# Splits moved from GpSimd to VectorE, memory rows asked for earlier, and a new timetable for cached values, in a decoder step

## The chip, the cores and the metric

One core of one Trainium2 chip. The metric is the device time of one execution, in microseconds (us). Five engines matter: TensorE (PE, matrix products; PEld is its weight loads), VectorE (DVE), ScalarE (ACT), GpSimd (POOL), and the sync engine (SP), which only issues transfers. ACT and POOL issue transfers too. Each engine works through its own list in order; semaphores tie the lists together.

## The reference, cut to what matters

The reference is one inference step of a one-layer hybrid decoder, for a prompt of 1,024 positions and for eight sample sequences of one new position each, with shared weights. Model width is 1,024, and there are four head groups of 256 columns.

```python
z = rmsnorm(x, g) @ w_in            # columns split among the groups below
outs = (fox(q, k, v, logf),         # A: causal, 4 heads of 64, decay bias
        sgu(u, v),                  # B: gated position mixing in chunks of 128
        dilated(q, k, v, rel_bias), # C: 3 dilated windows, 4 heads
        mem_attend(q, mk, mv))      # M: 4 heads into 256 memory tokens
x = x + merge_groups(outs) @ w_out
x = x + conv_ffn(rmsnorm(x, g))     # w_up, causal conv of width 3, silu gate, w_down
```

The memory keys and values are `rmsnorm(mem) @ w_mem_kv`. For each sample sequence, group A also reads 4,096 cached keys and values, 32 pages of 128 rows that a page table names; C reads 320 cached rows per sequence, and M 256. All data are float32.

## The kernel before, in words

**Products in three parts.** A float32 product is made of three products of "hi" and "lo" parts: `whi*hhi + wlo*hhi + whi*hlo` (lines 856 to 858, and 1035 to 1037 in the feed-forward part). ACT writes the hi part (a copy that rounds), another engine the lo part (value minus hi part).

**Stage 1, projection (0 to about 362 us).** Six column blocks of weights, 0 to 4 of `w_in` and 5 of `w_mem_kv`, each of eight chunks of 128 rows. PE works through units `(b, tt)`: block b with `tt` = "S" (the samples) or 0 to 7 (128 prompt positions), and (5, 0) and (5, 1) for the memory rows. Chunk q = 8b + kc is loaded by SP (`w_load`, line 454, which waits until chunk q - 4 is split, since there are four staging buffers), its hi part is made by ACT (`split_hi`, 1136) and its lo part, for q of 8 and more, by POOL (`split_lo`, 2162). `chunk_turns` (323) puts chunks 0 to 3 of block b at units (b-1, 0) to (b-1, 3) and chunks 4 to 7 all at (b-1, 7), where the units of that block free their slots. Beside this DVE normalises the q and k heads (`reduce_sq`, `finish_norm`, 1561, which waits for an inverse root from POOL), gates group B (`gate`, 1597), and multiplies cached keys by the sample queries (`k_dot`, lines 1546 and 1549, one "granule" of four pages at a time). A ring of four slots holds the granules of keys; SP and ACT load two pages each in this stage (`load_pages`, 353; lines 356 and 357 are the reading of a page number and the transfer). The memory rows (`memT`) are loaded in pairs at units (4, 2) to (4, 5) by `x_load` (462), which waits for the pair before to be split; ACT makes their hi part (1156), DVE their lo part (1520).

**Stage 2, attention (about 362 to 735 us).** 96 steps g, eight to a head: 0 to 31 causal heads, 32 to 63 memory heads, 64 to 95 dilated heads. A step is one block of 128 queries: PE makes the logits (931, 932), DVE adds a bias and takes the maximum (1795), ACT the exponential (`ex`, 1277), PE transposes (941, 946), ACT and DVE copy to SBUF (1289, 1811), PE multiplies with the values (957), and DVE divides (1820). In steps 0 to 15 DVE also has the last 16 key granules, whose four pages SP loads alone.

The cached values are summed by PE in between. `v_sum(k)` (961, matmuls at line 976) takes granule k of 74: 64 of four pages for A, and ten for C and M, loaded with one transfer each. They pass through a ring of four slots, so that granule k can be loaded once `v_sum(k - 4)` is done. `v_step` (414) is the timetable: which step has which granule. POOL's list is one loop over k (`v_load`, 2191): all four pages for k under V0, else two, and the other two come from SP at the step of `v_sum(k - 4)` (`V_PAIR`, 437; 617).

```python
V0, V1, V2 = 8, 28, 44      # granules 0-7: steps 4-15; 8-27: 16-31; 28-43: 32-63; 44-73: 64-86
```

POOL's loop also has four maxima over partitions (`max_all`, 2148) at fixed k and, at k = 66, an inverse root that waits for the squares of step 79 (`rs_o`). DVE waits for the second maximum in `subtract_a(1)` at step 19 (1643); its own part of that maximum is written in step 16.

**Stage 3 (735 us to the end).** Output projection and feed-forward part, with PE busy throughout; the change touches nothing in it.

Of the kernel before, what the change touches and what calls it, by code (L numbers as in the profile page):

```python
# [97 lines left out]
def build(nc, t):  # L98
# [5 lines left out]
    with ctx:  # L104
# [308 lines left out]
        V0, V1, V2 = 8, 28, 44  # L413
        v_step = [4 + k * 12 // V0 for k in range(V0)] + [16 + (k - V0) * 16 // (V1 - V0) for k in range(V0, V1)] + \
# [14 lines left out]
        def v_total(k):  # L429
            return sum(64 if n < V0 else 32 if n < NVA else 16 for n in range(k % 4, k + 1, 4))  # L430

        def v_total_sp(k):
            return sum(32 for n in range(k % 4, min(k + 1, NVA), 4) if n >= V0)
# [4 lines left out]
        for k_ in range(V0, NVA):  # L438
            V_PAIR.setdefault(v_step[k_ - 4], []).append(k_)
# [11 lines left out]
        def _(sp):  # L451
# [63 lines left out]
            for u, k in enumerate(units):  # L515
                b, tt = k
                for q in CT_load[u]:
                    w_load(q)
# [16 lines left out]
                if b == 4 and tt != "S" and tt >= 2 and tt < 6:  # L535
                    for i in (2 * (tt - 2), 2 * (tt - 2) + 1):
                        x_load(16 + i)
# [74 lines left out]
            for g in range(STEPS):  # L612
# [4 lines left out]
                for k in V_PAIR.get(g, ()):  # L617
                    sp.wait_ge(S("v_used"), k - 3)
                    load_pages(sp, vpool, k // 8, k % 8, k % 4, (2, 3), vring, "vs_ld")
# [515 lines left out]
        def _(act):  # L1135
# [187 lines left out]
            for g in range(STEPS + 4):  # L1323
# [8 lines left out]
                if g < STEPS:  # L1332
                    ex(g)
                if g == 2:
                    samp_exp(0)
# [137 lines left out]
        def _(dve):  # L1473
# [214 lines left out]
            for u, k in enumerate(units):  # L1688
                b, tt = k
                if b == 4 and tt != "S" and tt >= 2 and tt < 6:  # L1690
# [14 lines left out]
                if pending:  # L1705
                    finish_norm(pending)
                    pending = None
                for n in grans:
# [419 lines left out]
        def _(pool):  # L2128
# [33 lines left out]
            def split_lo(q):  # L2162

                pool.wait_ge(S("w_hi"), q + 1)
                pool.tensor_tensor(wlo[:, q % NW, 0:WID[q // KC]], wst[:, q % 4, 0:WID[q // KC]],  # L2165
                                   whi[:, q % NW, 0:WID[q // KC]].bitcast(f32), ALU.subtract).then_inc(S("w_split"), 1)
# [6 lines left out]
            for u, k in enumerate(units):  # L2173
                for bb, kc in CT[u]:
                    split_lo(bb * KC + kc)
# [15 lines left out]
            def v_load(k):  # L2191
                if k >= 4:
                    pool.wait_ge(S("v_used"), k - 3)
                if k < NVA:
                    load_pages(pool, vpool, k // 8, k % 8, k % 4, range(4) if k < V0 else (0, 1), vring, "vr_ld")
# [6 lines left out]
            for k in range(NV):  # L2202
                if k == 17:
                    max_all(2, 0, 16, 32)
                if k == 38:
                    max_all(3, 1, 0, 32)
                if k == 43:
# [72 lines left out]
```

## Time and profile before

| | |
|---|---|
| time before, three runs | 1625.07 us median (1620.05 to 1626.87) |
| the profiled execution's own time | 1638.29 us |
| its span, first to last instruction | 1635.5 us |
| granted TensorE clock, mean | 0.912 of full speed |
| busy: PE, PEld, DVE, ACT, POOL | 89%, 81%, 59%, 28%, 15% |
| moved by DMA | 172.90 MB, mean 106 GB/s |

The profiled execution took 13.2 us more than the median of the unprofiled ones. Times in the trace are counted from the first instruction. In a timeline row stand start, duration, engine, source line, operation, written and read tiles; in brackets how long the engine stood idle before it, and what ended that. `PE L856` is TensorE at line 856. PEclk is the granted clock of TensorE as a share of 2.4 GHz.

### The profile page before, as it was taken

The page shows a single profiled execution, that of the slowest core. Times are in us where ns is not written, and L with a number is a line of the kernel's source. Part 1 is how long each engine was busy: PE and PEld are TensorE (multiplying, and loading weights), DVE is VectorE, ACT ScalarE, POOL GpSimd, SP SyncE. Part 2 cuts the span into 40 slices and gives each one's busy share as a digit, 9 for nine tenths or more (in the row PEclk, how much of TensorE's full clock was granted, in tenths as well). Part 3 has the DMA queues.
Part 4 walks back from the last instruction along what each step waited for, and adds up shares of the span by engine and source line. Part 5 has one row for each costly group of instructions (what it writes and reads, how often), then busy time and mean ns, then how long its engine had stood idle before and what let it go on. Part 6 is the DMA issues. An engine that isn't in the chain of part 4 may idle for free.

```text
span 1635.5 us, 25981 instructions
## 1 busy us (share of the span) xinstructions
PE 1463.0 (89%) x8745; PEld 1320.4 (81%) x8745; DVE 959.1 (59%) x1490; ACT 461.9 (28%) x720; POOL 238.2 (15%) x293
## 2 busy tenths in 40 slices
PE   6985989746889798787989999999999999999997
PEld 4774777635666566577989999999999999999997
DVE  6566568646855856383456664555645556454653
ACT  5213112223334444452232321222212222221210
POOL 5533146142123213300000000000000000000000
PEclk8998989866678758898999999999999999999999
DMA  6277546437566846521300211202111020120202
GB/s 207 94 244 220 164 127 194 142 111 217 166 201 190 273 116 202 178 74 45 131 26 1 78 39 39 66 14 78 34 46 65 14 79 16 63 66 14 78 1 114
DMA packets 124745, 172.90 MB, mean 106 GB/s; under 512 B 22869, under 2 KB 97646, under 8 KB 124194
## 3 DMA queue, kind: packets, MB, share of 16 engines
q1 hardware_dynamic: 102864, 134.49, 26.2%
q0 software_dynamic: 8384, 24.13, 5.0%
q10 hardware_dynamic: 13354, 12.47, 2.5%
q8 instruction: 78, 1.28, 0.3%
q14 instruction: 65, 0.53, 0.1%
HBM read 157.09 MB, written 16.91 MB: 106 GB/s over the span
## 4 chain that ended last, share of the span: by engine, by line
PE 65%; DVE 7%; issue 6%; SPq 4%; DMA 3%; POOL 2%; ACT 2%; POOLq 0%; ACTq 0%; DVEq 0%; PEldq 0%
PE ps L1035 16%; PE ps L1036 16%; PE ps L1037 16%; PE ps L957 4%; SPq L356 2%; PE ps L856 2%; PE ps L858 2%; PE ps L857 2%; PE ps L976 2%; SPq L357 1%; DMA vring<-in_cache_a_v 1%; PE ps L941 1%; PE ps L908 1%; PE ps L932 1%; DVE ring L1546 1%
## 5 line engine op out<-in xcount | busy, mean ns | idle before, releaser
L1035 PE MATMUL ps<-hhi,uhi 128*128 128x344 f32 x1056 | 339.5, 322 | 12.4 <-DVE ulo L1996 5.0
L1036 PE MATMUL ps<-hlo,uhi 128*128 128x344 f32 x1056 | 338.7, 321 | 2.7 <-issue 2.7
L1037 PE MATMUL ps<-hhi,ulo 128*128 128x344 f32 x1056 | 338.1, 320 | 0.0
L1035 PEld LDWEIGHTS ps<-hhi,uhi 128*128 128x128 f32 x1056 | 199.7, 189 | 14.3 <-issue 11.2
L1036 PEld LDWEIGHTS ps<-hlo,uhi 128*128 128x128 f32 x1056 | 199.7, 189 | 3.9 <-issue 3.9
L1037 PEld LDWEIGHTS ps<-hhi,ulo 128*128 128x128 f32 x1056 | 199.7, 189 | 0.0
L856 PE MATMUL ps<-whi,hhi 128*128 128x512 f32 (+1 forms) x376 | 152.8, 406 | 44.7 <-POOL wlo L2165 31.0
L1035 PE MATMUL ps<-ahi,dhi 128*128 128x344 f32 x528 | 170.4, 323 | 3.6 <-DVE dlo L2121 3.6
L1036 PE MATMUL ps<-alo,dhi 128*128 128x344 f32 x528 | 170.5, 323 | 0.0
L1037 PE MATMUL ps<-ahi,dlo 128*128 128x344 f32 x528 | 169.7, 321 | 0.0
L2050 DVE TENSOR_TENSOR uu<-ps,rstd_bc 128x1032 f32<-128x1032 f32 x44 | 54.3, 1233 | 183.8 <-PE ps L1037 183.7
L957 PEld LDWEIGHTS ps<-vst,pts 128*128 128x128 f32 x704 | 107.8, 232 | 62.8 <-issue 33.8
L857 PE MATMUL ps<-wlo,hhi 128*128 128x512 f32 (+1 forms) x376 | 148.2, 394 | 0.0
L858 PE MATMUL ps<-whi,hlo 128*128 128x512 f32 (+1 forms) x376 | 148.0, 394 | 0.0
L957 PE MATMUL ps<-vst,pts 128*128 128x65 f32 x704 | 121.1, 323 | 20.4 <-DVE oN L1820 20.2
L856 PEld LDWEIGHTS ps<-whi,hhi 128*128 128x128 f32 x376 | 76.7, 204 | 65.4 <-POOL wlo L2165 34.9
L2083 DVE TENSOR_TENSOR x<-ps,x 128x1032 f32<-128x1032 f32 x80 | 98.3, 1229 | 13.0 <-PE ps L1037 10.7
L1546 DVE TENSOR_TENSOR ring<-ring,qb 128x1024 f32<-128x1024 f32 x64 | 83.0, 1297 | 38.4 <-DMA ring<-in_cache_a_k 38.4
L357 POOL DMA_DIRECT2D vring<-in_cache_a_v x144 | 77.9, 541 | 185.9 <-issue 163.2
L1035 PEld LDWEIGHTS ps<-ahi,dhi 128*128 128x128 f32 x528 | 100.2, 190 | 5.5 <-DVE dlo L2121 3.9
L1037 PEld LDWEIGHTS ps<-ahi,dlo 128*128 128x128 f32 x528 | 100.2, 190 | 0.0
L1036 PEld LDWEIGHTS ps<-alo,dhi 128*128 128x128 f32 x528 | 100.2, 190 | 0.0
(243 smaller groups left out, 2361.2 us busy)
## 6 DMA issues: line engine op xcount, KB each, us to landing
fst<-in_w_upL SPq DMA_DIRECT2D x44, 512.0 KB, 3.7
ring<-in_cache_a_k SPq DMA_DIRECT2D x168, 128.0 KB, 2.4
vring<-in_cache_a_v POOLq DMA_DIRECT2D x144, 128.0 KB, 3.0
vring<-in_cache_a_v SPq DMA_DIRECT2D x112, 128.0 KB, 2.7
ring<-in_cache_a_k ACTq DMA_DIRECT2D x88, 128.0 KB, 2.7
fst<-in_w_down SPq DMA_DIRECT2D x22, 512.0 KB, 3.6
wst<-in_w_in SPq DMA_DIRECT2D x32, 256.0 KB, 4.3
x<-in_xT SPq DMA_DIRECT2D x16, 258.0 KB, 4.9
```

Source lines behind the costliest of these rows:

```text
L356: page = sp.value_load(ptab[0:1, bass.ds(seq * PAGES + (group * 4 + j), 1)], min_val=0, max_val=NPOOL - 1)
L357: sp.dma_start(dst[:, slot, j, :], pool[bass.ds(page, 1)].rearrange("o p c -> p (o c)"))\
L856: pe.matmul(out, lh, whi[:, sl, 0:w], start=(kc == 0), stop=False)
L857: pe.matmul(out, lh, wlo[:, sl, 0:w], start=False, stop=False)
L858: i = pe.matmul(out, ll, whi[:, sl, 0:w], start=False, stop=(kc == KC - 1))
L957: i = pe.matmul(ps[:, 6, 0:HD + 1], pts[:, g % 2, j, :], vst[:, hp % 2, j, H % 2, :], start=(j == 0), stop=(j == nb - 1))
L1035: pe.matmul(out, lhs_hi(kc), rhs_hi(kc)[:, cs], start=(n == 0), stop=False)
L1036: pe.matmul(out, lhs_hi(kc), rhs_lo(kc)[:, cs], start=False, stop=False)
L1037: i = pe.matmul(out, lhs_lo(kc), rhs_hi(kc)[:, cs], start=False, stop=(n == nk - 1))
L1546: dve.tensor_tensor(kv, kv, q.broadcast_to([P, 4, WG]), ALU.mult).then_inc(S("k_mul"), 1)
L2050: dve.tensor_tensor(c3(uu[:, :]), U3(k % 2), c3(rstd_bc[:, :]), ALU.mult).then_inc(S("f_free"), 1)
L2083: dve.tensor_tensor(c3(x2[:, d, :]), U3(d % 2), c3(x2[:, d, :]), ALU.add).then_inc(S("f_free"), 1)
```

## The change

Three things. The lo parts of weight chunks 8 to 47 are made by VectorE, at the start of the unit, and in a block's last unit behind `finish_norm`. SP asks for the memory rows at the head of units (4, 2) to (4, 5), ahead of the weights. The timetable of cached values becomes: granules 0 to 11 in steps 4 to 15, 12 to 25 in steps 16 to 31, 26 to 33 in steps 32 to 63, 34 to 73 in steps 64 to 86; for granules 0 to 11 POOL loads two pages and ACT the other two, those of granules 0 to 3 in step 0. POOL's third and fourth maximum come at k = 33 and 36.

```diff
-        V0, V1, V2 = 8, 28, 44
-        v_step = [4 + k * 12 // V0 for k in range(V0)] + [16 + (k - V0) * 16 // (V1 - V0) for k in range(V0, V1)] + \
+        V0, V1, V2 = 12, 26, 34
+        v_step = [4 + k for k in range(V0)] + [16 + (k - V0) * 16 // (V1 - V0) for k in range(V0, V1)] + \
...
-        for k_ in range(V0, NVA):
-            V_PAIR.setdefault(v_step[k_ - 4], []).append(k_)
+        for k_ in range(NVA):
+            V_PAIR.setdefault(max(v_step[k_ - 4], 3) if k_ >= 4 else 0, []).append(k_)
... sync engine, projection
             for u, k in enumerate(units):
                 b, tt = k
+                if b == 4 and tt != "S" and tt >= 2 and tt < 6:
+                    for i in (2 * (tt - 2), 2 * (tt - 2) + 1):
+                        x_load(16 + i)
                 for q in CT_load[u]:
                     w_load(q)
...
-                if b == 4 and tt != "S" and tt >= 2 and tt < 6:
-                    for i in (2 * (tt - 2), 2 * (tt - 2) + 1):
-                        x_load(16 + i)
... sync engine, attention
                 for k in V_PAIR.get(g, ()):
-                    sp.wait_ge(S("v_used"), k - 3)
-                    load_pages(sp, vpool, k // 8, k % 8, k % 4, (2, 3), vring, "vs_ld")
+                    if k >= V0:
+                        sp.wait_ge(S("v_used"), k - 3)
+                        load_pages(sp, vpool, k // 8, k % 8, k % 4, (2, 3), vring, "vs_ld")
... scalar engine, attention
                 if g < STEPS:
                     ex(g)
+                for n in V_PAIR.get(g, ()):
+                    if n < V0:
+                        if n >= 4:
+                            T_.wait("v_used", n - 3)
+                        load_pages(act, vpool, n // 8, n % 8, n % 4, (2, 3), vring, "vs_ld")
... vector engine, projection
                 b, tt = k
+                if tt != NT - 1:
+                    for bb, kc in CT[u]:
+                        split_lo(bb * KC + kc)
...
                 if pending:
                     finish_norm(pending)
                     pending = None
+                if tt == NT - 1:
+                    for bb, kc in CT[u]:
+                        split_lo(bb * KC + kc)
                 for n in grans:
                     granule(n)
... gpsimd
             for u, k in enumerate(units):
-                for bb, kc in CT[u]:
-                    split_lo(bb * KC + kc)
...
-                    load_pages(pool, vpool, k // 8, k % 8, k % 4, range(4) if k < V0 else (0, 1), vring, "vr_ld")
+                    load_pages(pool, vpool, k // 8, k % 8, k % 4, (0, 1), vring, "vr_ld")
...
-                if k == 38:
+                if k == 33:
                     max_all(3, 1, 0, 32)
-                if k == 43:
+                if k == 36:
                     max_all(4, 2, 0, 32)
```

## Rows read from the trace of the kernel before

**Rows 1.** Busy time by stretch: from:to, length, busy (count) by engine, PEclk, DMA share, GB/s

```profile
50.00:362.00 312.00, 254.94 (x1142) 206.55 (x1141) 194.42 (x273) 64.65 (x129) 118.33 (x106) 0.89 0.54 165
395.00:453.00 58.00, 47.57 (x290) 36.99 (x291) 50.06 (x99) 22.10 (x39) 11.37 (x22) 0.71 0.58 172
453.00:476.00 23.00, 18.11 (x120) 13.57 (x119) 10.46 (x34) 6.76 (x10) 6.88 (x14) 0.77 0.81 231
476.00:520.00 44.00, 42.15 (x315) 31.48 (x315) 22.15 (x74) 20.66 (x37) 13.96 (x26) 0.81 0.55 172
520.00:609.00 89.00, 76.28 (x427) 53.38 (x423) 61.53 (x145) 42.96 (x122) 18.67 (x35) 0.70 0.67 202
609.00:671.00 62.00, 55.54 (x473) 40.53 (x473) 36.12 (x105) 32.82 (x67) 19.27 (x36) 0.91 0.65 194
880.00:1635.00 755.00, 738.75 (x4664) 734.40 (x4663) 423.58 (x503) 165.11 (x151) 0.00 (x0) 1.00 0.15 49
640.00:660.00 20.00, 17.40 (x156) 12.64 (x156) 12.21 (x36) 12.01 (x27) 8.85 (x16) 1.00 0.89 277
```

**Rows 2.** Waits of PE, 50 to 362 us: total, times, longest

```profile
PE ps L856 <- POOL wlo L2165: 31.0, 6, 14.3
PE ps L856 <- DVE zn L1570: 8.4, 2, 4.6
```

**Rows 3.** Splits by source line: DVE's eight of block 0, and POOL's 40 (min/median/max ns)

```profile
L1511 DVE TENSOR_TENSOR wlo<-wst,whi x8: 677/684/1777, 8.3 to 28.2; 128x512 fp32r<-128x512 f32 x8
L2165 POOL TENSOR_TENSOR wlo<-wst,whi x40: 725/1287/2275, 53.0 to 345.6; 128x512 fp32r<-128x512 f32 x32, 128x260 fp32r<-128x260 f32 x8
```

**Rows 4.** Timelines of DVE, POOL, ACT and PE around the ends of blocks

```profile
130.50 6.60 POOL L2165 TENSOR_TENSOR wlo<-wst,whi 128x512 fp32r<-128x512 f32 x4 [17.41 <-ACT whi L1145]
196.97 0.85 DVE L1605 SCALAR_TENSOR_TENSOR ob<-ps,prm_b,zo 128x64 f32<-128x64 f32 x4
339.45 0.19 POOL L2144 TENSOR_SCALAR rsn<-ssn 128x4 f32<-128x4 f32 x1 [7.62 <-issue]
340.83 0.48 DVE L1570 SCALAR_TENSOR_TENSOR zn<-ps,rsx,rsn 128x256 f32<-128x256 f32 x1 [5.67 <-POOL rsn L2147]
342.10 0.80 PE L856 MATMUL ps<-whi,hhi 128*128 128x512 f32 x1 [14.31 <-POOL wlo L2165]
```

**Rows 5.** SP's timeline at unit (4, 3)

```profile
289.37 0.42 SPq L501 DMA_DIRECT2D scr_q<-zo  x1
296.81 0.91 SPq L472 DMA_DIRECT2D xst<-in_memT  x2
```

**Rows 6.** Issues of pages by queue (min/median/max ns), and ScalarE's pair

```profile
L357 POOL DMA_DIRECT2D vring<-in_cache_a_v x144: 538/538/740, 360.5 to 657.0; - x144
144.45 1.44 ACTq L357 DMA_DIRECT2D ring<-in_cache_a_k  x2
493.50 0.54 POOL L357 DMA_DIRECT2D vring<-in_cache_a_v  x1 [0.62 <-issue]
```

**Rows 7.** DVE's timeline, steps 3 and 15

```profile
392.34 1.23 DVE L1546 TENSOR_TENSOR ring<-ring,qb 128x1024 f32<-128x1024 f32 x1 [10.89 <-DMA ring<-in_cache_a_k]
450.23 1.23 DVE L1546 TENSOR_TENSOR ring<-ring,qb 128x1024 f32<-128x1024 f32 x1 [2.38 <-DMA ring<-in_cache_a_k]
```

**Rows 8.** DVE and POOL around step 19

```profile
456.17 0.16 DVE L1640 TENSOR_TENSOR small<-small 8x16 f32<-8x16 f32 x1
473.88 0.39 POOL L2150 PARTITION_ALL_REDUCE small<-small  x1 [7.37 <-issue]
474.31 0.90 DVE L1648 TENSOR_TENSOR sA<-sA,small 128x128 f32<-128x128 f32 x4 [6.58 <-POOL small L2150]
```

**Rows 9.** PE's value sums: two that waited, and one at full clock

```profile
622.29 1.03 PE L976 MATMUL ps<-vring,sA 128*4 128x256 f32 x8 [3.18 <-DMA vring<-in_cache_a_v]
643.48 0.61 PE L976 MATMUL ps<-vring,sA 128*4 128x256 f32 x8
679.15 1.04 PE L976 MATMUL ps<-vring,sC 96*4 96x256 f32 x8 [7.77 <-DMA vring<-in_cache_c_v]
```

More of the change, by code:

```diff
@@ L429, in v_total @@
         def v_total(k):
-            return sum(64 if n < V0 else 32 if n < NVA else 16 for n in range(k % 4, k + 1, 4))
+            return sum(32 if n < NVA else 16 for n in range(k % 4, k + 1, 4))
         def v_total_sp(k):
-            return sum(32 for n in range(k % 4, min(k + 1, NVA), 4) if n >= V0)
+            return sum(32 for n in range(k % 4, min(k + 1, NVA), 4))
         def k_total(n):
@@ L2160, in x_add @@
                 pool.tensor_tensor(sacx[:, c], sacx[:, c], (sqt0 if i % 2 else sqt1)[:, :], ALU.add).then_inc(S("x_acc"), 1)
[L2162 to L2166, printed above, removed]
             for i in range(8):
```

## The prediction

> **What bounds the kernel now.** I read the table by stretches first. After 880 us TensorE is busy 738.75 of 755 us at full clock [rows 1]; the change touches nothing there, so what happens before has to be worth the difference. From 50 to 362 us (projection) TensorE is busy 254.9 of 312 us, and the list of its waits gives 31.0 us to the lo parts that GpSimd makes and 8.4 us to VectorE's normalising [rows 2]. In attention the bound changes by stretch [rows 1]: steps 4 to 15 (395 to 453 us) belong to VectorE, busy 50.1 of 58; steps 20 to 31 (476 to 520) and 64 to 79 (609 to 671) belong to TensorE, 42.2 of 44 and 55.5 of 62; the memory steps (520 to 609) to TensorE and VectorE in turn, 76.3 and 61.5 of 89, at a mean clock of 0.70, between its levels of 1.2 and 2.4 GHz. Three single waits stand out in the timelines: VectorE 10.89 us at step 3 for key pages [rows 7], VectorE 6.58 us at step 19 for a maximum from GpSimd [rows 8], TensorE 7.77 us at step 80 for a value granule [rows 9].
>
> **Projection: the splits.** The change moves 40 splits: 32 of 512 columns at 0.684 us on VectorE instead of 1.287 on GpSimd [rows 3], and 8 of 260 columns, which no VectorE row shows; I take half, 0.35. That is 32 x 0.684 + 8 x 0.35 = 24.7 us more for VectorE, busy 194.4 of 312 us [rows 1]. The splits for kc 0 to 3 fall in units where it has slack; I cost them at nothing. If the cover were gone, 16 x 0.684 + 4 x 0.35 = 12.3 us would show.
>
> The four chunks at a block's end do show. GpSimd needed 6.60 us for four [rows 4], VectorE needs 2.7; but in blocks 0, 3 and 4 they now stand behind `finish_norm`, some 2 us of VectorE work that itself waits for GpSimd's inverse root. So the first chunk comes later and the last one earlier. For the memory block: GpSimd is held by the first maximum over partitions until 339.45 (7.62 us of idle "issue" before its next row), VectorE gets its root and starts at 340.83, and the first split ends at 340.83 + 0.5 + 0.9 + 0.7 = 342.9; TensorE resumed at 342.10 [rows 4]. **Nearly all of the 14.3 us wait, the largest of the 31.0, therefore stays**, with another name on it. Its last chunk comes at 345 instead of 346.9: -1. Block 0 +1, block 3 0, block 1 (no `finish_norm`, first chunk as late as now, last 2 earlier) -2. In block 2 the four splits enter ahead of a gate that TensorE stands waiting for (VectorE row at 196.97 [rows 4]): +2.7. Ends of blocks: about +1.
>
> **Projection: the memory rows.** SP had nothing to do after 289.8 and asked for the second pair at 296.81 [rows 5], because the weight ahead of it waited for a split. Without that it goes out as soon as the first pair is split: up to 7 us earlier, of which VectorE's own added splits (four of block 3's end and two more) take some 3. I take -4, out of 0 to -7, and it comes off the 8.4 us wait and what follows it. Projection: **-3**.
>
> **Steps 0 to 15.** ScalarE gets 24 page issues. A pair takes 1.44 us from first to last [rows 6], so a page costs 1.44 - 0.35 = 1.1. Eight in step 0: 8.8 us, which delay the second exponential and with it the third bias row, but behind these VectorE waits 10.89 us for keys anyway [rows 7]: nothing. Queued behind the other 16 (2.2 us in each of steps 4 to 11) are ScalarE's copies and exponentials; it is busy 22.1 of 58 us, 39.7 with them, and VectorE stays the longer [rows 1]: +1. Four more sums on TensorE (4 x 0.97, below) fit beside VectorE: nothing. On SP the value pairs of steps 10 and 11, which stood ahead of the last key loads, go to steps 12 and later: the 2.38 us key wait of step 15 goes [rows 7]. Together **-1**.
>
> **Steps 16 to 31.** GpSimd reaches the second maximum after loading granule 16, for which it needs `v_sum(12)`: at step 19 now, at step 16 with the new timetable. VectorE's part was written at 456.17; the maximum came at 473.88, after 7.37 us of "issue" that start only when GpSimd gets there; VectorE waited until 474.31 [rows 8]. New: 456.3 + 7.4 + 0.4 = 464.1, and VectorE reaches its wait at about 462.7: 1.5 us are left of 6.6, so -5. Six sums fewer (20 to 14). One takes 0.61 us at full clock (0.55 until the next instruction) and 1.03 at half (0.97) [rows 9]; TensorE is the bound at a clock of 0.81: 6 x 0.75 = -4.5. Without the stop, less of the stretch runs at 1.2 GHz: -1.5. Together **-11**.
>
> **Memory steps.** Eight sums fewer. About three fall where VectorE's products of cached rows set the pace, and count nothing; five count 0.97: **-5**.
>
> **Dilated steps.** Granules 34 to 63 are due in steps 64 to 80, where 44 to 65 were. Four lie ready; 26 must come. GpSimd issues a page every 0.54 + 0.62 = 1.16 us [rows 6], two per granule: 26 x 2.32 = 60.3, plus about 4.6 until the last one lands and 3 for unevenness: 68 us against 62. TensorE by itself: 55.5 + 9 x 0.55 = 60.5 [rows 1, 9], so the loads are the bound and the sums hide behind them: +6. Now the stop at step 80: granule 66 waits behind an inverse root that needs step 79. Its sum moves from step 80 to 82; that gives two steps of about 3.2 us: of 7.77 us [rows 9] 1.5 stay, -6. Dilated: **0**.
>
> The page "DMA: Bandwidth & Descriptors" of the Trainium skill says under "Issuing engines are not separate DMA queues" that all queues run on the same 16 DMA engines, so that one more issuing engine saves only sequencer time. By this rule ScalarE's 24 issues bring no value earlier; I credited them with nothing, so the sum is the same, but the rule makes a rival, below.
>
> **Sum.** -3 - 1 - 11 - 5 + 0 = -20. The profiled execution took 1638.3 us, 13.2 over the median of 1625.1: 1618 of 1638, and taken off the median **1605 us**.
>
> **Rivals.**
>
> *A. The maximum stays late* (chance 0.14). The step -5 - 1.5 fails if GpSimd's 7.4 us land behind more loads, or if the granules it then loads late stop TensorE in steps 21 to 23. For it: from 464.1 each of three granules takes 2.3 us and is due within 3 us. Against: four slots are filled before. 1605 + 6.5 = 1612.
>
> *B. ScalarE's issues are exposed* (0.13). They sit between exponentials on a chain from VectorE to TensorE and back. If nothing hid them, 24 x 1.1 = 26 us; half of that gives 1617, all of it 1630. For it: in steps 4 to 7 ScalarE would be busy some 4.7 us of a step of 4.5. Against: VectorE's 50.1 of 58.
>
> *C. Dilated heads bound by transfers* (0.12), the case on the slower side. Thirty granules of 524 KB are 15.7 MB, plus some 2.5 MB for the next heads. In 68 us that is 268 GB/s; the trace shows 277 in one stretch of 20 us, 194 over the whole of steps 64 to 79 [rows 1]. If a granule took 3.3 us, as over steps 16 to 31 (67 us for 20), these steps would last 30 x 3.3 = 99 us: +37 instead of +6, thus 1605 + 31 = 1636. It decides from (62 + 26 + 8) / 30 = 3.2 us a granule, 26 being what the rest gains. For it: waits of 3.18 us already stand there [rows 9]. Against: GpSimd held 2.3 us a granule for eight granules at 277 GB/s. The rule cited above is what this rival rests on beside the rows: three queues, but one set of engines.
>
> *D. More clock* (0.06). The memory steps have a clock of 0.70 and the projection 0.89; if the stops vanish and 2.4 GHz holds, another 15 us go: 1590.
>
> **Chances and range.** Forecast 0.55 (its own range 1596 to 1612). What a measurement of this kernel can tell from no change is about 0.5%, 8.1 us: faster is under 1617, slower over 1633. Forecast and D are faster; of A 0.11 faster, 0.03 the same; of B 0.01, 0.09 and 0.03 slower; of C 0.03 the same and 0.09 slower. Faster 0.73, same 0.15, slower 0.12. Range: downwards the unknown costs (memory rows -3 more, step 19 -2, memory steps -3, part of D) reach 1592; upwards A and most of B are to be held (hidden splits +12, issues +13): 1627.
>
> **What would show it.** No PE wait on GpSimd's splits; a wait of some 14 us at the memory block under VectorE's name; the second `xst` issue within 3 us of the first pair's split; the second maximum some 8 us after step 16's row and VectorE's wait at step 19 under 3 us; steps 16 to 31 in about 56 us instead of 67; the memory steps in 84 instead of 89; steps 64 to 79 in about 68 with GpSimd issuing without a gap; the wait at `vring<-in_cache_c_v` under 2 us. Wrong if VectorE waits for ScalarE in steps 4 to 11 by more than 5 us in sum, or if steps 64 to 79 take over 75 us.

## The result, and the profile after

The changed kernel takes **1635.1 us** (median of 12 runs, 1631.5 to 1644.5) beside 1627.5 us of the kernel before on the same chip (12 runs, 1620.1 to 1631.0): ratio **1.0055, interval 1.0034 to 1.0076**. It is slower, by about 9 us; 1605 was forecast. The profiled execution has a span of 1642.9 us (before 1635.5) and a mean clock of 0.907 (before 0.912).

The table by stretches, cut at the starts of steps 4, 16, 32, 64, 74, 80 and 87 (a step starts with VectorE's first instruction on its logits); columns as in [rows 1]:

```profile
50.00:362.00 312.00, 251.09 (x1145) 204.98 (x1143) 207.02 (x315) 67.59 (x133) 66.78 (x68) 0.90 0.55 167
390.59:444.78 54.19, 43.68 (x302) 31.79 (x306) 49.70 (x98) 22.31 (x39) 12.02 (x22) 0.79 0.73 217
444.78:494.52 49.74, 48.86 (x404) 37.71 (x400) 32.85 (x106) 27.07 (x47) 15.49 (x29) 0.92 0.72 219
494.52:587.51 92.99, 85.42 (x371) 63.61 (x368) 62.11 (x146) 43.06 (x121) 9.49 (x18) 0.53 0.48 144
587.51:627.44 39.93, 34.59 (x320) 23.20 (x313) 24.93 (x68) 19.15 (x34) 17.70 (x33) 0.97 0.76 220
627.44:661.48 34.04, 28.04 (x205) 21.25 (x209) 11.34 (x37) 14.04 (x33) 11.67 (x21) 0.75 0.71 209
661.48:712.05 50.57, 36.04 (x235) 25.80 (x229) 16.53 (x48) 15.12 (x26) 10.41 (x10) 0.66 0.38 105
```

TensorE's waits, 50 to 362 us, against [rows 2]: the low parts still hold it, now under VectorE's name; the positional gate (`ob`) and the forget row (`crow`) hold it longer than before (6.2 and 5.5 us).

```profile
PE ps L857 <- DVE wlo L1517: 30.2, 3, 15.5
PE ps L832 <- DVE ob L1611: 9.2, 3, 4.4
PE ps L832 <- DVE crow L1750: 9.0, 1, 9.0
```

The timelines that answer to [rows 4] (memory block), [rows 8] (steps 16 to 19) and [rows 9] (here step 82); `osqj` is ScalarE's square of step 79, which the inverse root waits for:

```profile
338.69 0.19 POOL L2156 TENSOR_SCALAR rsn<-ssn 128x4 f32<-128x4 f32 x1 [7.41 <-issue]
340.99 2.49 DVE L1517 TENSOR_TENSOR wlo<-wst,whi 128x512 fp32r<-128x512 f32 x4
341.73 0.79 PE L857 MATMUL ps<-whi,hhi 128*128 128x512 f32 x1 [15.55 <-DVE wlo L1517]
...
455.56 0.39 POOL L2162 PARTITION_ALL_REDUCE small<-small  x1 [7.18 <-issue]
458.68 0.89 DVE L1654 TENSOR_TENSOR sA<-sA,small 128x128 f32<-128x128 f32 x4
...
659.65 0.40 ACT L1319 ACTIVATE osqj<-oN 128x256 f32<-128x256 f32 x1
659.64 1.49 POOL L383 DMA_DIRECT2D vring<-in_cache_c_v  x2
670.31 0.20 POOL L2156 TENSOR_SCALAR rso<-sso 128x24 f32<-128x24 f32 x1 [9.19 <-issue]
679.07 1.04 PE L977 MATMUL ps<-vring,sC 96*4 96x256 f32 x8 [5.67 <-DMA vring<-in_cache_c_v]
```

Where the time went, by the starts of steps in the two traces: step 0 starts 2.6 us earlier than before, step 16 7.8, step 32 25.0 and step 74 still 22.8 us earlier. Then it is lost: step 80 is 9.4 us earlier, step 87 is 4.8 us later, and the last instruction 7.4. **Steps 64 to 86 take 124.5 us, before 97.9.**

That 97.9 is itself high. The profiled execution before was 13 us over its median and has in step 67 a stop that is longer than in any other trace (11.57 us for the step; 8.02 and 6.62 in e3 and e4, about 4 to 5 in the rest). The two versions below with the old timetable take 92.9 and 92.7 us for steps 64 to 86. So the dilated heads lost about 32 us, where I had forecast none.

### The profile page after: what moved, and what is told of

The parts are those of the page before. It is cut to its first block, busy times and chain, and to the rows that moved or that the text cites. A ratio compares the mean times of both kernels' runs of the same rounds, so it can differ in the third digit from the quotient of the medians.

```text
span 1642.9 us, 25988 instructions
## 1 busy us (share of the span) xinstructions
PE 1465.6 (89%) x8745; PEld 1325.1 (81%) x8745; DVE 970.6 (59%) x1530; ACT 462.9 (28%) x720; POOL 177.7 (11%) x237
## 3 DMA queue, kind: packets, MB, share of 16 engines
q1 hardware_dynamic: 101712, 133.44, 25.9%
## 4 chain that ended last, share of the span: by engine, by line
PE 65%; DVE 8%; issue 6%; SPq 5%; DMA 3%; POOL 2%; ACT 1%; POOLq 0%; ACTq 0%; DVEq 0%; PEldq 0%
PE ps L1036 17%; PE ps L1037 16%; PE ps L1038 16%; PE ps L958 4%; SPq L356 2%; SPq L357 2%; PE ps L977 1%; PE ps L857 1%; PE ps L858 1%; PE ps L859 1%; PE ps L942 1%; PE ps L933 1%; DVE ring L1552 1%; DMA vring<-in_cache_a_v 1%; PE ps L909 1%
## 5 line engine op out<-in xcount | busy, mean ns | idle before, releaser
L2062 DVE TENSOR_TENSOR uu<-ps,rstd_bc 128x1032 f32<-128x1032 f32 x44 | 54.2, 1233 | 188.2 <-PE ps L1038 188.2
L958 PEld LDWEIGHTS ps<-vst,pts 128*128 128x128 f32 x704 | 108.5, 233 | 52.8 <-issue 34.7
L857 PEld LDWEIGHTS ps<-whi,hhi 128*128 128x128 f32 x376 | 75.7, 201 | 57.1 <-DVE wlo L1517 38.2
L2095 DVE TENSOR_TENSOR x<-ps,x 128x1032 f32<-128x1032 f32 x80 | 98.3, 1229 | 14.3 <-PE ps L1038 11.9
L357 POOL DMA_DIRECT2D vring<-in_cache_a_v x128 | 69.4, 542 | 198.3 <-issue 177.4
L1552 DVE TENSOR_TENSOR ring<-ring,qb 128x1024 f32<-128x1024 f32 x64 | 78.0, 1219 | 17.0 <-DMA ring<-in_cache_a_k 16.9
```

The lines of the kernel that those rows point to most:

```text
L357: sp.dma_start(dst[:, slot, j, :], pool[bass.ds(page, 1)].rearrange("o p c -> p (o c)"))\
L857: pe.matmul(out, lh, whi[:, sl, 0:w], start=(kc == 0), stop=False)
L958: i = pe.matmul(ps[:, 6, 0:HD + 1], pts[:, g % 2, j, :], vst[:, hp % 2, j, H % 2, :], start=(j == 0), stop=(j == nb - 1))
L1552: dve.tensor_tensor(kv, kv, q.broadcast_to([P, 4, WG]), ALU.mult).then_inc(S("k_mul"), 1)
L2062: dve.tensor_tensor(c3(uu[:, :]), U3(k % 2), c3(rstd_bc[:, :]), ALU.mult).then_inc(S("f_free"), 1)
L2095: dve.tensor_tensor(c3(x2[:, d, :]), U3(d % 2), c3(x2[:, d, :]), ALU.add).then_inc(S("f_free"), 1)
```

## The experiments

Lengths in us of groups of steps in each run's trace, with the granules of values in the dilated heads, and the time as a ratio to the kernel before, timed beside it on the same chip (95% interval in brackets; e1 to e4, e5 to e8, e9 to e12, e13 to e16 and e17 to e18 share a chip each):

| version | granules | 4-15 | 16-31 | 32-63 | 64-73 | 74-79 | 80-86 | ratio |
|---|---|---|---|---|---|---|---|---|
| before | 20 | 57.6 | 66.9 | 89.8 | 40.9 | 20.6 | 36.4 | 1 |
| after | 30 | 54.2 | 49.7 | 93.0 | 39.9 | 34.0 | 50.6 | 1.0055 |
| e1 | 20 | 56.2 | 49.6 | 84.5 | 34.5 | 23.3 | 37.6 | 0.9892 (0.9843-0.9940) |
| e2 | 30 | 57.1 | 49.2 | 89.6 | 39.6 | 34.6 | 46.8 | 1.0077 (1.0046-1.0107) |
| e3 | 20 | 58.0 | 68.9 | 84.2 | 36.6 | 20.1 | 36.2 | 1.0039 (1.0005-1.0072) |
| e4 | 20 | 57.5 | 68.5 | 87.1 | 35.0 | 19.9 | 37.8 | 0.9955 (0.9929-0.9981) |
| e5 | 20 | 56.1 | 50.7 | 86.8 | 35.4 | 21.7 | 38.9 | 0.9844 (0.9795-0.9893) |
| e6 | 30 | 60.0 | 49.3 | 88.8 | 42.0 | 32.8 | 40.1 | 1.0007 (0.9984-1.0030) |
| e7 | 30, half the bytes | 56.5 | 49.3 | 88.5 | 45.2 | 23.7 | 47.4 | 0.9972 (0.9946-0.9998) |
| e8 | 30 | 56.5 | 49.6 | 90.0 | 55.4 | 34.7 | 48.0 | 1.0144 (1.0106-1.0182) |
| e9 | 30, no pages | 56.0 | 49.4 | 91.6 | 34.3 | 25.9 | 44.7 | 0.9895 (0.9852-0.9938) |
| e10 | 30, a quarter of the sums of 24 of them | 55.1 | 50.5 | 89.3 | 40.0 | 34.6 | 47.8 | 1.0016 (0.9990-1.0041) |
| e11 | 20 | 56.8 | 49.6 | 86.7 | 33.6 | 21.7 | 37.7 | 0.9813 (0.9768-0.9858) |
| e12 | 30 | 55.7 | 49.3 | 89.3 | 42.2 | 35.4 | 47.2 | 1.0017 (0.9992-1.0042) |
| e13 | 30, half the requests | 55.2 | 50.1 | 88.4 | 34.1 | 34.3 | 43.9 | 0.9995 (0.9966-1.0024) |
| e14 | 20 | 55.6 | 49.4 | 88.6 | 35.9 | 26.5 | 27.7 | 0.9718 (0.9677-0.9760) |
| e15 | 16 | 56.0 | 50.5 | 88.0 | 30.5 | 20.1 | 21.9 | **0.9675** (0.9637-0.9714) |
| e16 | 30 | 54.1 | 48.9 | 90.5 | 42.5 | 32.3 | 47.6 | 1.0018 (0.9997-1.0039) |
| e17 | 12 | 54.7 | 49.9 | 95.4 | 30.3 | 19.0 | 25.5 | 0.9741 (0.9697-0.9784) |
| e18 | 16 | 56.1 | 49.9 | 83.7 | 30.5 | 20.4 | 21.7 | 0.9718 (0.9684-0.9752) |

How far one trace can be trusted can be read there too: nine executions with the same projection start step 0 between 358.1 and 364.7 us. A difference of three microseconds in a single trace says nothing. The changed kernel's own trace is the latest of the nine; their mean is 361.8, and 367.4 in the kernel before.

**1. Which part of the change costs.** The changed kernel with the dilated heads' share of before (e1), and each of the three parts alone on the kernel before (e2, e3, e4; their diffs are parts of the change's own).

```diff
 e1, on the changed kernel
-        V0, V1, V2 = 12, 26, 34
+        V0, V1, V2 = 12, 28, 44
-                if k == 33:        # third maximum
+                if k == 38:
-                if k == 36:        # fourth maximum
+                if k == 43:
```

> The changed kernel with V0, V1, V2 = 12, 28, 44 and the last two maxima back ahead of granules 38 and 43: the dilated heads get 20 granules and the memory heads 16, as before the change; all else of the change stays. Theory 1 (the dilated heads are overloaded: 30 granules where 20 were): step 64 starts 20 to 22 us earlier than before the change, steps 64 to 86 take the 97.9 us of before instead of 124.5, and the time is 18 to 22 us under the kernel before (ratio 0.987 to 0.989). Theory 2 (TensorE's granted clock takes back later whatever the early steps gain): steps 64 to 86 still take 115 us or more, and the time is within 6 us of the kernel before (ratio 0.996 to 1.004).

> The kernel before with the new timetable alone (12, 26, 34, ScalarE's page issues, the maxima ahead of granules 33 and 36); splits stay on GpSimd and memory rows behind the weights. Theory 1 (the timetable alone makes the loss): step 4 starts within 1 us of the kernel before (395.1), steps 4 to 31 gain about 20, steps 64 to 86 lose about 26, and the time is 10 to 14 us over the kernel before (ratio 1.006 to 1.009). Theory 3 (the splits on VectorE or the earlier memory rows cost what the timetable gains): the time is under the kernel before.

> The kernel before with only the 40 splits moved to VectorE. By the prediction's terms: ends of blocks +1, the wait of 14.3 us at the memory block stays under VectorE's name; time within 3 us of the kernel before (ratio 0.998 to 1.002). If VectorE's 24.7 us more are not hidden: 12 us over it (ratio 1.007).

> The kernel before with only the memory rows asked for ahead of the weights. By the prediction's term: step 0 starts 4 us earlier (0 to 7), time 1 to 5 us under the kernel before (ratio 0.997 to 0.999), since the attention behind it can take some back. Rival: nothing, because the weight that is now asked for behind the rows comes late in their place.

e1 takes 1605.6 us, by the ratio 18 less than the kernel before, and steps 64 to 86 take 95.4 us. The mean clock is the highest of these four (0.927): the clock takes back nothing that was gained early, and theory 2 is out. e2 has the whole loss, 1.0077. By ratios of 1626 us the parts alone are +12.5 (timetable), +6.3 (splits) and -7.3 (rows), in sum +11.5 beside the +9 of the change.

Both projection terms were off. In e4 SP asks for the second pair of memory rows at 285.46 instead of 296.81 [rows 5], and step 0 starts 10.6 us earlier. In e3 the price was not the amount of VectorE's work (it is busy 203 of the 306 us from 50 to 356), but its **order**: a split stands at the head of a unit and waits for ScalarE's high part, and what TensorE needs waits behind it. VectorE's timeline around the forget row, first e3, then e4:

```profile
159.97 0.69 DVE L1511 TENSOR_TENSOR wlo<-wst,whi 128x512 fp32r<-128x512 f32 x1 [3.60 <-ACT whi L1145]
...
162.96 0.27 DVE L1744 TENSOR_TENSOR crow<-ps,crow 32x128 fp32r<-32x128 f32 x1
```

```profile
159.65 0.28 DVE L1738 TENSOR_TENSOR crow<-ps,crow 32x128 fp32r<-32x128 f32 x1 [2.48 <-ACT crow L1256]
```

In e4 the split is in GpSimd's list, and VectorE waits for nothing but the row's own input. From before to e3 TensorE's waits grow by 3.5 us for the row, 3.0 for the gates, 1.8 for the bias (0.8 to 2.6) and 0.7 for the low parts, and shrink by 2.5 for the normalised rows and 0.4 for the queries: 6.1 in all, against 6.3 by the ratio. But the traces do not show that this reaches the end of the stage: SP asks for the first pair of memory rows at 290.10 in e3 and 285.74 before, 4.4 us late, and step 0 starts only 0.2 us late. So the rows show what waits, the ratio what it costs, and the way from one to the other stays open.

**2. Whether the gains add up, and what stops TensorE at steps 80 to 86.** The splits go back and e1's timetable stays (e5); and, on the changed kernel, one tiny instruction makes GpSimd change its program early (e6).

```diff
 e6
                 if k == 36:
                     max_all(4, 2, 0, 32)
+                    pool.wait_ge(S("gmax"), 4)
+                    pool.tensor_scalar(rso[32:64, 35:36], nhalf[32:64, 0:1], 1.0, 0.0, ALU.mult, ALU.add).then_inc(S("pool_chain"), 1)
+                    chain[0] += 1
                 if k == 66:
+                    pool.wait_ge(S("pool_chain"), chain[0])
```

> Memory rows ahead of the weights and the timetable with V0, V1, V2 = 12, 28, 44 (20 granules in the dilated heads), splits back on GpSimd: what the first four runs say is good, and nothing else. If the gains add up (step 0 10 us earlier as in the run with the rows alone, and from there the 27 us of the run with more in the memory heads): step 0 at 357, step 87 at 667 to 672, time 23 to 28 us under the kernel before (ratio 0.983 to 0.986). Rival: the splits on VectorE were part of that gain, then no better than the 0.989 of that run.

> The changed kernel with one tiny TENSOR_SCALAR on GpSimd right behind its last maximum over partitions, 100 us before the inverse root of the outputs. Theory 4 (the 9.19 us of idle issue ahead of the inverse root at 670.31 are GpSimd's change from one kind of program to the other, which starts only when it gets there, since ScalarE's square was done at 660.2): the root starts within 1 us of the last load ahead of it (661), the next cached rows are asked for at 666 instead of 675, the wait of 5.67 us at step 82 goes, steps 81 to 86 take some 10 us less than 43, time 7 to 12 us under the changed kernel (ratio to before 0.998 to 1.001). Rival (the idle time is the queue or the transfers): it stays over 7 us.

e5: 1604.2 us, ratio 0.9844, within what was expected if the gains add up (step 87 at 675.6 is 4 us later than expected). e6's mechanism was right as well: the 9.19 us of idle ahead of the inverse root are gone, they stand (7.13) in front of the tiny instruction, where nobody waits, and the cached rows go out in time. GpSimd in e6:

```profile
572.00 0.18 POOL L2215 TENSOR_SCALAR rso<-nhalf 32x1 f32<-32x1 f32 x1 [7.13 <-issue]
...
662.22 1.49 POOL L383 DMA_DIRECT2D vring<-in_cache_c_v  x2
663.78 0.20 POOL L2156 TENSOR_SCALAR rso<-sso 128x24 f32<-128x24 f32 x1
...
668.25 1.52 POOL L383 DMA_DIRECT2D vring<-in_cache_c_v  x2
```

Steps 80 to 86 fall from 50.6 to 40.1 us (other versions with 30 granules and their value pages: 46.8 to 48.0, and 43.9 in e13), the time from 1.0055 to 1.0007. So GpSimd idles when it goes from a maximum over partitions to arithmetic or back, with page requests in between or not: 7.62 and 7.37 us in [rows 4, 8], 5.6 to 10.2 in the runs. Where the program is already there, the second maximum starts 1.12 to 1.15 us after VectorE's release (six versions below).

The Trainium skill's page "GPSIMD Engine Reference", section "2.1 Instruction dispatch", has a load of code of about 6 us at the first call of a freshly loaded kernel, with no instruction to be seen in the profile. The trace agrees in that no instruction shows, and the size here is 5.6 to 10.2 us; that the idle time is such a load no run shows.

How exposed this is depends on when GpSimd gets there. In the kernel before it had made its last request by 662.99 and then waited for step 79 as well:

```profile
669.36 0.19 ACT L1318 ACTIVATION_READ_ACCUMULATOR osqj<-oN 128x1 f32 x1
670.37 0.20 POOL L2144 TENSOR_SCALAR rso<-sso 128x24 f32<-128x24 f32 x1 [7.38 <-ACT osqj L1318]
```

The square is done at 669.55 and the root starts 0.82 us later: change of program and wait lie side by side. In the changed kernel the square is done at 660.15, GpSimd gets there at 661.13, and the 9.19 us stand alone.

**3. What is late in steps 64 to 79: the sums, the bytes or the requests.** Five versions of the changed kernel (the semaphore totals that go with each edit are not shown).

```diff
 e7: SP's two pages of granules 34 to 63 left out
-                    if k >= V0:
+                    if V0 <= k < V2:
 e8: GpSimd one page, SP three
+  (2, 3) if k < V2 else (1, 2, 3)          # SP
+  (0, 1) if k < V2 else (0,)               # GpSimd
 e9: no pages for granules 34 to 63, on both queues
+                if V2 <= k < NVA:
+                    pass
 e10: one matmul of four for granules 40 to 63
+                    if q == 3 or not 40 <= k < NVA:
 e13: one request for two neighbouring pages, from each queue
+            page = (4 * k + j) % (NPOOL - 2)
+            eng.dma_start(vring[:, k % 4, j:j + 2, :], vpool[page:page + 2].rearrange("o p c -> p o c"))
```

> The changed kernel without SP's two pages of each granule in the dilated heads (30 granules, 60 pages, 7.9 MB); TensorE sums what lies in the slots. Left out: half of the cached values of granules 34 to 63, so that the rows of the samples are not the reference's. Theory 5 (transfers bind: 216 GB/s and half as much again in peaks): steps 64 to 86 fall from 124.5 to under 108 us. Theory 6 (GpSimd's own issues bind, 1.155 us a page and two pages a granule): GpSimd asks as often as ever, steps 64 to 86 stay within 5 us of 124.5.

> The changed kernel, but in the dilated heads GpSimd asks for one page of each granule and SP for three; the bytes stay. Theory 6 (GpSimd's issues bind): steps 64 to 86 fall under 112 us. Theory 5 (transfers bind): they stay over 119 us. If neither is the bound but the ring of four slots, each to be summed before it is asked for again, both runs give about half of the gain.

> The changed kernel without the pages of granules 34 to 63 on both queues (120 pages, 15.7 MB); TensorE sums old values in the slots, and all waits but those for these pages stay. Left out: the cached values of the dilated heads' 30 granules, so the rows of the samples are not the reference's. If late pages cause the loss (issue, transfer or ring, whichever): steps 64 to 79 take 56 to 60 us instead of 74, with TensorE's clock near 1.0, and steps 64 to 86 take 95 to 105 us instead of 124.5. If the 10 more sums themselves cause it: steps 64 to 86 stay over 115 us.

> The changed kernel with one of the four matmuls of each value sum for granules 40 to 63 (steps 67 to 80); all pages are loaded and waited for. Left out: three quarters of these sums, so the rows of the samples are not the reference's. 24 granules of 0.41 to 0.73 us less is 10 to 17 us less work for TensorE. If late pages set the pace: steps 64 to 86 fall by less than 5 us from 124.5. If TensorE's own work does: by 10 us or more.

> The changed kernel, but for granules 34 to 63 each queue asks once for two neighbouring pages (at fixed places of the cache) instead of twice for one: the same 15.7 MB, 60 requests instead of 120. The rows of the samples are not the reference's, since other pages are summed. Theory 6 (the requests set the pace): steps 64 to 79 take 58 to 64 us instead of 74, near the 60.2 of the run without loads, and the time falls by 10 us or more (ratio to before 0.999 or less). Theory 5 (the transfers do): steps 64 to 79 stay over 70 us.

Late pages are the cause: without them (e9) steps 64 to 86 take 104.9 us, and the time is 26 us under the changed kernel's. With a quarter of the sums of granules 40 to 63 (e10) they take 122.4: the sums do hide, as forecast.

e7 (116.2 us for steps 64 to 86) decided for neither theory, e8 (138.1) met the words of "transfers bind" with the bytes unchanged, and e13 (68.4 for steps 64 to 79) fell between its two cases, since I had asked of the whole stretch. Split at step 74 the runs agree. The rows of steps 64 to 73 and 74 to 79, in e7:

```profile
584.09:629.27 45.18, 37.93 (x324) 26.46 (x321) 24.97 (x67) 19.26 (x34) 18.62 (x35) 0.85 0.50 145
629.27:652.98 23.71, 20.95 (x205) 15.26 (x202) 11.34 (x37) 13.87 (x33) 10.11 (x20) 1.00 0.37 108
```

in e9:

```profile
584.94:619.20 34.26, 33.97 (x324) 24.30 (x321) 24.92 (x68) 18.84 (x34) 0.00 (x0) 0.95 0.24 62
619.20:645.15 25.95, 24.00 (x205) 17.82 (x201) 11.23 (x37) 14.07 (x34) 1.51 (x2) 0.87 0.10 28
```

and in e13, with four microseconds of the second stretch:

```profile
581.52:615.65 34.13, 33.05 (x324) 23.50 (x321) 24.93 (x68) 18.84 (x34) 12.97 (x18) 0.99 0.84 265
615.65:649.94 34.29, 27.20 (x205) 20.34 (x201) 11.25 (x38) 14.20 (x34) 7.26 (x10) 0.80 0.70 223
...
620.00:624.00 4.00, 0.40 (x7) 0.14 (x8) 0.84 (x3) 1.23 (x3) 0.00 (x0) 0.89 1.06 363
```

**Steps 64 to 73 are held by the requests.** Half of them bring the stretch from 39.9 to 34.1 us, as fast as no pages at all (34.3), and move 265 GB/s instead of 220; half the bytes bring nothing (45.2). In the changed kernel GpSimd asks from 589.7 to 632 us every 1.16 us, never idle for more than 0.9. SP, too, needs 17.52 us for 16 pages, 1.10 each:

```profile
606.90 17.52 SPq L357 DMA_DIRECT2D vring<-in_cache_a_v  x16
```

In e8 SP has three pages of each granule, 3.3 us, and the stretch takes 55.4. I had added up GpSimd's pace alone; the second queue is as slow, and a granule is ready when the later queue is. One thing e13 does not separate: its places in the cache are fixed, so the reading of a page number, the 0.62 us ahead of each 0.54, goes together with every second request.

**Steps 74 to 79 are held by the transfers.** There the next head pair's queries, keys and bias rows (0.5 MB each) share the DMA engines. With half the requests the stretch stays at 34.3 us, with half the bytes it takes 23.7; in e13 the DMA engines are full from 616 to 624 us (share 1.10 and 1.06, 324 and 363 GB/s), while TensorE is busy 0.40 of four microseconds. In the changed kernel they are full from 630 to 639, and TensorE waits 2.22 us for a page; then its matmuls run at half the clock:

```profile
633.00:636.00 3.00, 0.91 (x4) 0.63 (x2) 1.32 (x4) 0.99 (x2) 0.53 (x1) 0.50 1.07 345
639.00:642.00 3.00, 3.00 (x16) 3.00 (x16) 0.45 (x2) 0.33 (x1) 1.07 (x2) 0.50 0.79 229
```

So most of the 34 us are not spent with full DMA engines (mean share 0.71, clock 0.75): the jam starts the stop, and the low clock makes it long. The kernel before had the same requests in the same steps and ran on at full clock:

```profile
646.52 0.44 SPq L512 DMA_DIRECT2D qst<-scr_q  x1
653.19 0.96 SPq L578 DMA_DIRECT2D toeC<-scr_t  x1
```

By the Trainium skill's page "DMA: Bandwidth & Descriptors", section "Issuing engines are not separate DMA queues", more issuing engines save sequencer time only. The trace agrees on both sides of it: up to step 73 that sequencer time is the bound, from step 74 on halving the requests brought nothing (34.3 beside 34.0 us).

**4. What else GpSimd's changes of program cost.** e12 is the changed kernel with the first maximum moved out of the projection; e11 is e5 with that and e6's instruction; e14 is e11 with the inverse root behind the cached rows.

```diff
 e11, e12
-                if k == (4, 5):
-                    max_all(1, 0, 0, 16)
+                if k == 4:                        # GpSimd's loop over granules
+                    pool.wait_ge(S("q_ones"), 1)
+                    max_all(1, 0, 0, 16)
-                if k == (4, 6):                   # VectorE
-                    subtract_a(0)
+                if g == 2:
+                    subtract_a(0)
 e14
-                if k == 66:
+                if k == 70:
```

> Rows first, splits on GpSimd, timetable 12, 28, 44 (0.9844 of the kernel before), and with it GpSimd's program changed 100 us ahead of the inverse root, and the first maximum over partitions moved from unit (4, 5) of the projection to behind the fourth granule of values, subtracted in step 2. If GpSimd's changes of program cost what the traces say (7.4 us twice in the projection inside a TensorE wait of 14.3, 7.2 at step 16, 9 at step 80): 8 us and 12 us less, ratio 0.971 to 0.977, 1582 to 1590 us. Rival: the waits for keys at steps 2 and 3 (10.9 and 11.8 us) take back the earlier start, then 0.978 to 0.982.

> The changed kernel with only the first maximum over partitions moved from unit (4, 5) to behind the fourth granule of values, subtracted in step 2. If the wait of 15.5 us of TensorE for the low parts at the memory block comes from GpSimd's two changes of program around that maximum: it falls under 8 us, step 0 starts 7 to 10 us earlier, and the time is 6 to 10 us under the changed kernel (ratio to before 0.999 to 1.002). Rival (VectorE's added splits make that wait): it stays over 12 us and the time stays at 1.0055.

> The fastest version so far (0.9813) with the inverse root of the outputs behind granule 69 instead of ahead of granule 66, so that the cached rows are asked for before GpSimd waits for step 79. The stop of 7.16 us at step 80 falls under 2 us, steps 80 to 86 take 29 to 33 us instead of 37.7; up to 2 us come back where the memory rows are then late. Ratio to before 0.975 to 0.979. If the stop was the landing of these rows and not GpSimd's turn, it stays over 5 us.

e12: step 0 starts 8.6 us earlier (5.7 against the mean of the nine above) and the time is 1.0017 instead of 1.0055. The longest wait for low parts falls from 15.5 to 9.5 us, not under 8:

```profile
PE ps L857 <- DVE wlo L1517: 21.5, 3, 9.5
```

In e11, too, step 0 starts 9.4 us earlier than in e5, and the keys of steps 2 and 3 take none of it back (steps 0 to 3 take 26.8 and 26.4 us). The second maximum, with the program already there, starts 1.14 us after VectorE's release. By the ratios e11, at 0.9813 and not 0.971 to 0.977, is only 5 us better than e5 (by the spans of the two profiled executions 15; the intervals allow both), and e6's gain is missing in it: steps 80 to 86 are as long as ever. With 20 granules GpSimd reaches the inverse root early and then waits there for step 79, with its program changed or not, and TensorE stopped 7.16 us for the rows behind it. e14 takes that away. GpSimd asks for the last cached rows, and only then comes the root:

```profile
635.80 0.68 POOL L383 DMA_DIRECT2D vring<-in_cache_c_v  x1 [2.44 <-PE ps L977]
636.55 0.20 POOL L2150 TENSOR_SCALAR rso<-sso 128x24 f32<-128x24 f32 x1
```

Steps 80 to 86 take 27.7 us instead of 37.7, ratio 0.9718; steps 74 to 79 take 26.5 instead of 21.7 in this trace, at a clock of 0.73.

**5. How many granules the dilated heads bear, and two leftovers.** e15 and e17 are e14 with V2 = 48 and 52 (maxima ahead of granules 40 and 46, 42 and 49). e16 puts ScalarE's requests back on GpSimd in the changed kernel. e18 is e15 with the splits on VectorE.

```diff
 e16, in ScalarE's step
-                for n in V_PAIR.get(g, ()):
-                    if n < V0: ... load_pages(act, vpool, ..., (2, 3), vring, "vs_ld")
 e16, in GpSimd's v_load
-  (0, 1)
+  range(4) if k < V0 else (0, 1)
```

> The version of e14_root_behind_rows with V0, V1, V2 = 12, 28, 48: 16 granules in the dilated heads and 20 in the memory heads, maxima ahead of granules 40 and 46. Four sums move from steps in which TensorE is the bound into steps that VectorE and TensorE share. If the dilated heads are still held by pages: 2 to 5 us under e14_root_behind_rows. If with 20 granules they are bound by TensorE alone (clock 1.00, no wait over 1.6 us): within 2 us of it.

> The changed kernel with the 24 page requests of ScalarE back on GpSimd (four pages of each of the first 12 granules). If ScalarE's issues neither cost nor bring anything, as the prediction has it: within 2 us of the changed kernel, provided GpSimd's 4.6 us a granule keep up with steps of 4.5 us; if they do not, granules 8 to 11 come late and steps 4 to 15 take 3 to 8 us more than 54.2, with a wait of TensorE for value pages. If ScalarE's issues were a cost: steps 4 to 15 get shorter.

> The version with V0, V1, V2 = 12, 28, 48 (0.9675) with 52 instead of 48: 12 granules in the dilated heads, 24 in the memory heads. If the pages no longer hold the dilated heads with 16 granules: four more sums cost in the memory steps what they save behind them, within 3 us of 0.9675. If they still do: 3 us or more faster. If the memory heads, at a clock of 0.69 and 228 GB/s, now become what is held by pages: 3 us or more slower.

> The version with V0, V1, V2 = 12, 28, 48 (0.9675) with the 40 splits on VectorE, as the change has them. By the waits that grew in every version with these splits (forget row 5.5 to 9.0 us, gates 4.8 or 6.2 to 9.2, bias 0.8 to 2.6, low parts 28.5 to 21 to 30): 5 to 8 us slower, ratio 0.971 to 0.973. If the splits cost nothing, as forecast: within 2 us of 0.9675.

e15 is **the fastest version, 1577.3 us, 52 under the kernel before**; it is 7 us better than e14 by the ratios, where 2 to 5 were expected. Behind step 64 TensorE is hardly ever stopped, at full clock:

```profile
575.12:605.61 30.49, 30.02 (x276) 22.43 (x273) 24.65 (x67) 18.25 (x33) 11.81 (x22) 1.00 0.71 198
605.61:625.68 20.07, 19.29 (x181) 14.77 (x178) 11.34 (x38) 14.57 (x35) 6.44 (x10) 1.00 0.87 253
625.68:647.54 21.86, 21.27 (x195) 16.67 (x188) 16.09 (x49) 13.89 (x24) 6.38 (x5) 1.00 0.39 124
```

e17 is 1.0068 times that, with intervals that overlap: moving four more granules out saves only 1.3 us in steps 64 to 79, and in its trace 7.4 are lost in the memory steps and 3.6 behind step 80. e16: steps 4 to 15 take 54.1 us beside 54.2, so ScalarE's issues show no cost there; other versions with these issues took up to 60.0 us, so a few microseconds could not be seen. Its time is nevertheless 6 us below the changed kernel's, and so is e10's, whose dilated steps are only 2 us shorter. The changed kernel was not timed beside them. Whether the 4 to 6 us lie in that stays open, and it bears on the ratios of e6 and e12 as well: beside e10 and e16 they show hardly a gain, and the case of both rests on their rows. e18 is 1.0044 times e15, as e1 is 1.0049 times e5 and e3 1.0039 times the kernel before. Each pair alone is near its uncertainty; three of them together say that the splits cost 6 to 8 us. The single traces do not confirm it: step 0 starts 0.2 us later with the splits in the first pair, 2.4 later in e1 and 0.8 earlier in e18, and all three spans with them are the shorter ones.

## Why the prediction was wrong

Forecast 1605, range to 1627, chance of slower 0.12; measured 1635.

- **Projection, -3 forecast.** Step 0 came 2.6 us earlier in this trace (5.6 by the mean of nine), but the number is luck: by the ratios of the parts, two errors cancel, rows -7.3 instead of -4 (at my bound of -7), splits +6.3 instead of +1. The step "the splits for kc 0 to 3 fall in units where it has slack; I cost them at nothing" failed. I had weighed busy time and not what waits behind a waiting instruction. Right was that nearly all of the 14.3 us wait stays under VectorE's name (15.5), and why; e12 shows it.
- **Steps 0 to 15, -1.** The trace has -5, about half of it within the scatter of traces. ScalarE's issues were hidden: rival B's 12 to 25 us are out by e16.
- **Steps 16 to 31, -11 forecast, -17.2 measured.** The maximum was there 11.2 us after the start of step 16 (by my sum 11.5), and VectorE found it ready. The stop at step 19 is gone, rival A with it. The excess over my sum is in steps 28 and 29, which took 13.5 us before and 6.5 after.
- **Memory steps, -5 forecast, +3.2 measured.** Eight sums fewer did not shorten them: ten traces with 8 granules have 88.4 to 93.0 us (mean 89.9), seven with 16 have 84.2 to 89.8 (mean 86.8). TensorE has 64 matmuls less and is busy longer, 85.4 us instead of 77.1, because the granted clock is 0.53 instead of 0.70 (0.53 to 0.62 in the ten traces, 0.65 to 0.76 in the seven). The step "five count 0.97" failed: it held the clock fixed. That the clock falls *because* those matmuls are gone is my reading; no run separates it.
- **Dilated steps, 0 forecast, +26.7 measured (32 against the other traces of the old timetable).** This decides the sign, and both halves failed: steps 64 to 79 took 12.5 us more where I had +6, steps 80 to 86 took 14.2 more where I had -6. "26 x 2.32 + 7.6 = 68 us" took one queue's pace and an undisturbed landing. It also counted to step 80 and was set beside 62 us that end with step 79; by then 28 granules are due, and the same sum gives 63. It was 74.0: 39.9 where two queues make requests at 1.1 us a page, 34.0 where the transfers of the next head pair come on top and the clock falls behind the stop.
- **The stop, "of 7.77 us 1.5 stay", -6.** I moved the sum two steps back and left GpSimd's side as it was: a root that waits for step 79. That wait was real, but a change of program lay beside it, of the length in [rows 4, 8] that I had called "issue" and gave no price here. With 30 granules GpSimd gets to the root only when step 79 is done; the change then starts, 9.19 us of idle time, and moves the stop from step 80 to 82. There 5.67 us of waiting stay, and 2.74 for the next granule. e6 shows it: steps 80 to 86 take 40.1 us instead of 50.6.
- **Rival C** had the right side, a wrong price and only a part of the mechanism. It put 99 us on steps 64 to 79, where 74.0 were measured, and rested on transfers alone, which hold in six of sixteen steps; that its 1636 is near the measured 1635 is luck. Against it I had that GpSimd once held its pace at 277 GB/s. That stretch contained the next heads' requests too, as the rows above show, so it was a fair test for 20 granules; it said nothing of a list in which both queues are never idle.
- **The range.** Its upper end, 1627, is less than its own terms give (1605 + 12 + 13 = 1630); the measured time lies above both.

## What to carry to other kernels

Count the requests of every queue that fills a buffer, and look at what else the DMA engines carry in just that stretch: here one stretch was held by the request pace in its first ten steps and by bytes in the next six, and only runs that halved each of them separately showed it. Moving work to an engine with slack costs nothing only if it does not wait there: a split that waits for another engine belongs behind what others need, or on an engine whose list nobody waits for. And idle time of a fixed length ahead of one kind of GpSimd instruction is a price of changing kinds: put kinds together, or make the change with a tiny instruction where nobody waits.

## What was unexpected of the hardware

- GpSimd's change between a maximum over partitions and arithmetic costs 5.6 to 8.0 us in most places (9.4 once) and 8.0 to 10.2 us ahead of the inverse root of the versions with 30 granules; heavy DMA traffic is not needed for the longer ones, since e9, without the pages, has 8.48. In the kernel before it stands in TensorE's path at the memory block and at step 19. At step 80 it lies beside the wait for step 79 and adds 0.8 us; with the change made early (e11) TensorE still waited 7.16 us there.
- TensorE took longer for less: 371 matmul records in 93.0 us at a clock of 0.53, where 435 took 89.8 at 0.70, and 467 took 88.0 at 0.69 in e15.
- Two neighbouring pages in one request take GpSimd 0.72 us to issue; one page takes 0.54, and where its number is read first another 0.62. The price is mostly per request.
